# A decoder layer on eight cores: bf16 chunks at multiples of 64 bytes, and conditioning blocks spread through the merge

## What is computed

```
ada = silu(c) @ w_ada + b_ada            # shift1, scale1, gate1, shift2, scale2, gate2
h   = rmsnorm(x, g_pre1) * (1 + scale1) + shift1
z   = h @ w_in                           # pool 1024 | lru 2048 | pool gate 2048 | lru gate 2048
y_pool = (window mean - u_pool) @ w_grp * scale ; y_lru = rglru(causal conv(u_lru))
merged = sigmoid(g_pool) * (y_pool @ w_pool_up) + sigmoid(g_lru) * (y_lru @ w_lru_up)
x   = x + gate1 * rmsnorm(merged @ w_out, g_post1)
h   = rmsnorm(x, g_pre2) * (1 + scale2) + shift2
up  = causal conv3(h @ w_ffn_up)         # 2 x 6144
x   = x + gate2 * rmsnorm((gelu(up_gate) * up_value) @ w_ffn_down, g_post2)
```

## Time and profile before

| | |
|---|---|
| time of three runs | 2472.26, 2476.87, 2477.47 us |
| the profiled execution | 2471.48 us |
| its span, slowest core (core 4) | 2469.9 us |
| spans of the eight cores | 2461.9 to 2469.9 us |
| PE busy | 2202.4 us (89%) |
| DVE, ACT busy | 1067.3 us (43%), 916.7 us (37%) |
| bytes moved by DMA | 338.42 MB, 137 GB/s |

### The profile page before, as it was taken

How to read it: one execution, slowest core, us unless ns; L and a number is a source line. 1 busy time by engine, 2 the same in 40 slices (tenths; PEclk the granted TensorE clock), 3 DMA queues, 4 the chain that set the end, 5 groups by cost and what they waited for, 6 DMA issues and landing times.

```text
span 2469.9 us, 41807 instructions; the slowest of 8 cores (2461.9 to 2469.9 us)
## 1 busy us (share of the span) xinstructions
PE 2202.4 (89%) x16574; PEld 1136.6 (46%) x16896; DVE 1067.3 (43%) x2195; ACT 916.7 (37%) x1232; POOL 146.5 (6%) x281
## 2 busy tenths in 40 slices
PE   2447888898888999999899999999999999999995
PEld 0122444444444555555445555555555555555552
DVE  0356988997311111111337666540005776563003
ACT  2446878885200000002364455440104444442101
POOL 0000000000000000000000000000000000000000
PEclk8568999999999999999999999999999999999997
DMA  9994656564265555658989976669877996778983
GB/s 226 250 163 77 107 100 110 90 114 96 52 111 101 105 94 96 110 104 148 180 177 192 187 142 130 128 131 184 132 128 146 199 172 134 137 137 162 199 134 96
DMA packets 61967, 338.42 MB, mean 137 GB/s; under 512 B 7504, under 2 KB 8016, under 8 KB 28240
## 3 DMA queue, kind: packets, MB, share of 16 engines
q0 software_dynamic: 39888, 273.17, 63.7%
q1 hardware_dynamic: 21888, 62.56, 7.8%
HBM read 586.69 MB, written 22.17 MB: 247 GB/s over the span
## 4 chain that ended last, share of the span: by engine, by line
PE 80%; ACT 7%; DMA 5%; DVE 5%; issue 3%; DVEq 0%; ACTq 0%; SPq 0%; POOLq 0%
PE ps_all L253 80%; ACT sb_R L230 6%; DMA sb_w<-w_ada 3%; DVE sb_R L236 2%; DVE sb_R L233 2%; DMA sb_R<-xp 1%; DMA sb_w<-w_lru_up 1%; ACT L230 1%; DVE sb_R L256 0%; ACT sb_rstd L230 0%; DVE sb_R L247 0%; DVEq L145 0%; ACT sb_wsm L230 0%; DVE sb_R L241 0%; DVE sb_mod L243 0%
## 5 line engine op out<-in xcount | busy, mean ns | idle before, releaser
L253 PE MATMUL ps_all<-sb_R,sb_w 128*128 128x512 bf16 (+4 forms) x14293 | 2032.8, 300 | 51.5 <-DMA sb_w<-w_lru_up 17.9
L253 PEld LDWEIGHTS ps_all<-sb_R,sb_w 128*128 128x128 bf16 x14592 | 1039.0, 98 | 1029.8 <-issue 62.9
L230 ACT ACTIVATE sb_R<-ps_all 128x128 f32<-128x128 f32 (+6 forms) x416 | 213.4, 546 | 662.3 <-PE ps_all L253 589.4
L236 DVE SCALAR_TENSOR_TENSOR sb_R<-sb_R,sb_cvec 128x450 f32<-128x450 f32 (+3 forms) x576 | 379.0, 703 | 26.8 <-ACT sb_R L230 15.2
L233 DVE TENSOR_TENSOR sb_R<-sb_R 128x577 bf16<-128x577 f32 (+9 forms) x148 | 166.0, 1121 | 169.5 <-ACT sb_R L230 153.2
L230 ACT ACTIVATE sb_R<-sb_R 128x578 f32<-128x578 f32 (+9 forms) x216 | 207.2, 981 | 78.3 <-DMA sb_R<-xp 44.1
L230 ACT ACTIVATE sb_wsm<-ps_all 128x577 bf16<-128x577 f32 (+1 forms) x64 | 42.0, 656 | 431.7 <-PE ps_all L253 431.2
L230 ACT ACTIVATE sb_R<-ps_all,sb_cvec 128x577 f32<-128x577 f32 (+4 forms) x184 | 170.4, 928 | 22.3 <-DVE sb_R L233 15.3
L233 DVE TENSOR_TENSOR sb_R<-sb_R,sb_mod 128x128 f32<-128x128 f32 x96 | 27.9, 290 | 297.8 <-ACT sb_R L230 294.5
L243 DVE TENSOR_SCALAR sb_mod<-ps_all,sb_cvec 128x17 f32<-128x17 f32 x96 | 18.0, 228 | 318.3 <-PE ps_all L253 317.6
L233 DVE TENSOR_TENSOR sb_R<-sb_R,sb_rstd 128x577 f32<-128x577 f32 (+5 forms) x128 | 119.9, 961 | 9.3 <-ACT sb_rstd L230 9.3
(11 more groups left out here) (57 smaller groups left out, 702.2 us busy)
## 6 DMA issues: line engine op xcount, KB each, us to landing
sb_w<-w_ffn_up POOLq DMA_DIRECT2D x96, 1024.0 KB, 9.9
sb_w<-w_ada POOLq DMA_DIRECT2D x48, 1024.0 KB, 15.4
sb_w<-w_ffn_down POOLq DMA_DIRECT2D x48, 1024.0 KB, 10.4
sb_w<-w_in POOLq DMA_DIRECT2D x36, 1024.0 KB, 11.3
sb_w<-w_out POOLq DMA_DIRECT2D x16, 1024.0 KB, 10.2
sb_R<-xm SPq DMA_DIRECT2D x4, 2312.0 KB, 91.9
sb_R<-xp SPq DMA_DIRECT2D x4, 2048.0 KB, 42.3
sb_w<-w_lru_up POOLq DMA_DIRECT2D x8, 1024.0 KB, 7.7
```

The costliest lines, as they stand in the source:

```text
L230: return self.P.op("act", lambda e: e.activation(out=out, in_=in_, func=func, **kw), after)
L236: return self.P.op("dve", lambda e: e.scalar_tensor_tensor(out=out, in0=in0, scalar=scalar, in1=in1, op0=op0, op1=op1), after)
L253: return self.P.op("pe", lambda e: e.matmul(out, lhsT=lhsT, rhs=rhs, start=start, stop=stop), after, signal)
```

## The change

Three edits.

1. Every bf16 view gets a stride that is a multiple of 64 bytes: SNB = 1184 elements (2368 bytes) in place of 1156, and SBB = 608 elements (1216 bytes) in place of 578. The offsets of the arena are moved so that all bf16 views start at multiples of 64; `R` itself moves to the front of SBUF (byte 16768 = 64 x 262) with the weight slots and `sb_wsm` behind it, all at multiples of 64. fp32 views keep their strides. The one operand that does not start at 64 is half B in the output projection: it reads `merged` from column 577, so at 2 bytes past a multiple of 64 (before: at 2 or 10 bytes past a multiple of 16). 256 of the 5120 pairs are of that kind.
2. To make room, `hist_up` moves into the tile `sth`, whose store to DRAM then has to be done first (`t_sth_out` is added to the waits of FFN up A, and `ffree` to those of the copies into `hist_up`), and of the four `x1s` buffers three instead of two lie in the first region.
3. In the merge, one ada block is run before the second gates block of a round, and one (two in round 3) between `w_lru_up` and `w_pool_up`, in place of three or two in a row behind the gates. In all it is 17 blocks as before.

```
+SNB = 1184
+SBB = 608
 O_HM = 0
-O_XM = O_HM + 4 * SN
+O_XM = 5568
+O_AG = 16 * 2 * SNB
+O_WGRP = O_AG + 8 * 4 * SN
+O_YLRU = O_WGRP + 4096
...
-O_YLRU = O_HP
...
+for o_bf in (O_HM, O_YLRU, O_HP, O_SQ, O_XCB, O_DB, O_YPOOL, O_MERGED, O_H2A, O_H2B, O_FLO, O_FHI):
+    assert o_bf % 64 == 0
...
+            self.R = self.sb("R", [128, R_BYTES // 4], F32)
+            self.wslots = [self.sb("w%d" % i, [128, 16, 256], BF16) for i in range(4)]
+            self.wsm = [self.sb("wsm%d" % i, [128, 2, 2, 256], BF16) for i in range(2)]
...
-            self.hist_up = self.sb("hist_up", [128, 96, 2], F32)
...
+            self.hist_up = self.sth[:].rearrange("p c s -> p (c s)")[:, 0:192].rearrange("p (c t) -> p c t", t=2)
...
-        hm = self.bfv(O_HM, 16, SN)
+        hm = self.bfv(O_HM, 16, SNB)
...
-        merged = self.bfv(O_MERGED, 16, SN)
+        merged = self.bfv(O_MERGED, 16, SNB)
...
+            self.ada_step()
             tg.update(self.gates(12 + q, 0, prev))
-            self.ada_step(3 if q < 2 else 2)
...
                     self.release(b, 3, [tg[bi + j]])
+                if bi:
+                    self.ada_step(2 if q == 3 else 1)
...
-                      h2=self.bfv(O_H2A, 16, SB_), halo=HALO, y0=0, t_g=[None] * DK, t_d=[None] * DK),
+                      h2=self.bfv(O_H2A, 16, SBB), halo=HALO, y0=0, t_g=[None] * DK, t_d=[None] * DK),
...
-        f_lo = self.bfv(O_FLO, 32, SB_)
-        f_hi = self.bfv(O_FHI, 16, SB_)
+        f_lo = self.bfv(O_FLO, 32, SBB)
+        f_hi = self.bfv(O_FHI, 16, SBB)
...
-                        keep.append(self.Vcopy(self.hist_up[:, chn, :], U[:, npr:npr + 2], evs[gv]))
+                        keep.append(self.Vcopy(self.hist_up[:, chn, :], U[:, npr:npr + 2], evs[gv] + ffree))
...
-        ftA = ffn_up("A", Ring([0, 2, 4]), nB, lambda jf: 1, [self.t_merge, halves["A"]["t_o"], self.t_stl_out])
+        ftA = ffn_up("A", Ring([0, 2, 4]), nB, lambda jf: 1, [self.t_merge, halves["A"]["t_o"], self.t_stl_out, self.t_sth_out])
...
-        x1s = [self.f32(O_X1ST + i * 4 * SB_, SB_) for i in range(2)]
-        x1s += [self.f32(O_X1SU + i * 4 * SB_, SB_) for i in range(2)]
+        x1s = [self.f32(O_X1ST + i * 4 * SB_, SB_) for i in range(3)] + [self.f32(O_X1SU, SB_)]
```

More of the change, by code:

```diff
@@ L51 @@
 O_SQ = O_XP + 16 * 4 * SP_
-O_AG = 16 * 2 * SN
-O_WGRP = O_AG + 8 * 4 * SN
-O_YLRU = O_HP
 SU = 1208
-O_U = O_YLRU + 16 * 2 * SN
+O_U = O_YLRU + 16 * 2 * SNB
 O_XC = O_U + 2 * 4 * SU
 O_XCB = O_XC + 4 * 4 * SN
-R_BYTES = O_XCB + 4 * 2 * SN
-O_YPOOL = O_AG + 4 * 4 * SN
 O_STP = O_AG
-O_DB = O_AG + 2 * 4 * SN
+O_DB = O_STP + 8 * SEQS * 15 * 4
+O_YPOOL = O_WGRP - 8 * 2 * SNB
 PU = 15 + NPR + SEQS * 23
-O_PU = O_YLRU + 16 * 2 * SN
+O_PU = O_U
 O_PS = O_PU + 4 * 4 * PU
 O_GB = O_AG
-O_MERGED = O_YLRU + 16 * 2 * SN
+O_GB3 = O_YPOOL - 4 * SN
+O_MERGED = O_U
+R_BYTES = O_MERGED + 16 * 2 * SNB
 O_OA = 0
@@ L70 @@
 O_H2A = 2 * 16 * 4 * SB_
-O_H2B = O_H2A + 16 * 2 * SB_
+O_H2B = O_H2A + 16 * 2 * SBB
 NXST = 6
-O_XST = O_H2B + 2 * 2 * SB_
-O_FLO = O_MERGED
+O_XST = O_H2B + 2 * 2 * SBB
+O_FLO = R_BYTES - 32 * 2 * SBB
 O_FHI = 0
 FU = 612
-O_FU0 = 16 * 2 * SB_
+O_FU0 = 16 * 2 * SBB
 O_D = O_OB
@@ L80 @@
 O_X1ST = O_STF + 96 * 32 * 4
-O_X1SU = O_H2B + 16 * 2 * SB_
+O_X1SU = O_H2B + 16 * 2 * SBB
 O_X1B = O_H2A
[L83 to L88, removed]
+for o_bf in (O_HM, O_YLRU, O_HP, O_SQ, O_XCB, O_DB, O_YPOOL, O_MERGED, O_H2A, O_H2B, O_FLO, O_FHI):
+    assert o_bf % 64 == 0
+for k_hm in range(16):
+    assert O_HM + 2 * SNB * (k_hm + 1) <= O_XM + 4 * SN * (k_hm // 2)
+assert O_SQ + 2 * 2 * SNB <= R_BYTES and O_XCB + 4 * 2 * SNB <= R_BYTES
+assert O_HP + 16 * 2 * SP_ <= O_U
+assert O_DB + 2 * 2 * SNB <= O_GB3 and O_PS + 2 * 4 * PU <= R_BYTES
+assert O_GB + 2 * 4 * SN <= O_GB3
+assert O_XST + NXST * 4 * SB_ <= O_X1SU and O_X1SU + 4 * SB_ <= O_MERGED and O_X1SU + 4 * SB_ <= O_FLO
+assert O_X1ST + 3 * 4 * SB_ <= O_H2B and O_X1B + 16 * 4 * SB_ <= O_FLO
 class Prog:
@@ L353, in build @@
             self.sth = self.sb("sth", [128, 16, SEQS], F32)
-            self.R = self.sb("R", [128, R_BYTES // 4], F32)
-            self.wslots = [self.sb("w%d" % i, [128, 16, 256], BF16) for i in range(4)]
+            self.hist_up = self.sth[:].rearrange("p c s -> p (c s)")[:, 0:192].rearrange("p (c t) -> p c t", t=2)
             self.w_sem = [P.new_sem("wsem%d" % i) for i in range(4)]
@@ L360, in build @@
             self.w_rot = 4
-            self.wsm = [self.sb("wsm%d" % i, [128, 2, 2, 256], BF16) for i in range(2)]
             self.wsm_sem = [P.new_sem("wsmsem%d" % i) for i in range(2)]
@@ L446, in front @@
         self.t_dv = self.Vts(self.dv[:, 3, :], self.dv[:, 2, :], 0.5, None, ALU.mult, after=[tv])
-        sq = [self.bfv(O_SQ + i * 2 * SN, 1, SN)[:, 0, :] for i in range(2)]
+        sq = [self.bfv(O_SQ + i * 2 * SNB, 1, SNB)[:, 0, :] for i in range(2)]
         sq_free = [None, None]
         hp = self.bfv(O_HP, 16, SP_)
-        hm = self.bfv(O_HM, 16, SN)
+        hm = self.bfv(O_HM, 16, SNB)
         self.hp, self.hm = hp, hm
@@ L597, in lru @@
         xc = [self.f32v(O_XC + s * 2 * 4 * SN, 2, SN) for s in range(2)]
-        xcb = [self.bfv(O_XCB + s * 2 * 2 * SN, 2, SN) for s in range(2)]
+        xcb = [self.bfv(O_XCB + s * 2 * 2 * SNB, 2, SNB) for s in range(2)]
         av = [self.f32v(O_AG + s * 4 * 4 * SN, 2, SN) for s in range(2)]
         gv = [self.f32v(O_AG + s * 4 * 4 * SN + 2 * 4 * SN, 2, SN) for s in range(2)]
-        y_lru = self.bfv(O_YLRU, 16, SN)
+        y_lru = self.bfv(O_YLRU, 16, SNB)
         self.y_lru = y_lru
@@ L795, in lru @@
         self.store(self.o_lh_p, self.h_carry[:], self.t_lru)
-        self.store(self.o_lh_s, self.sth[:], self.t_lru)
+        self.t_sth_out = self.store(self.o_lh_s, self.sth[:], self.t_lru)
     def pool_first(self, half_free, rows_free):
@@ L806, in pool_first @@
         S = [self.f32(O_PS + s * 4 * PU, PU) for s in range(2)]
-        db = self.bfv(O_DB, 2, SN)
+        db = self.bfv(O_DB, 2, SNB)
         stp = self.f32(O_STP, 8 * SEQS * 15).rearrange("p (c s t) -> p c s t", c=8, s=SEQS)
-        y_pool = self.bfv(O_YPOOL, 8, SN)
+        y_pool = self.bfv(O_YPOOL, 8, SNB)
         self.y_pool = y_pool
@@ L934, in merge_first @@
     def merge_first(self):
-        self.gb = [self.f32(O_GB, SN), self.f32(O_GB + 4 * SN, SN), self.rstd[:], self.f32(O_GB + 3 * 4 * SN, SN)]
+        self.gb = [self.f32(O_GB, SN), self.f32(O_GB + 4 * SN, SN), self.rstd[:], self.f32(O_GB3, SN)]
         self.merge_ring = Ring([0, 3])
@@ L1006, in ffn @@
         xst_cnt = [0] * NXST
-        sqn = self.bfv(O_H2B, 2, SB_)
+        sqn = self.bfv(O_H2B, 2, SBB)
         sqm = {"buf": sqb, "i": 0, "free": [None, None]}
@@ L1237, in ffn_up @@
                 H["stf_out"] = self.store(self.o_fconv_s, stf, H["t_up"])
-                self.store(self.o_fconv_p, self.hist_up[:], H["t_up"])
+                self.store(self.o_fconv_p, self.hist_up, H["t_up"])
             return ft
```

2 lines of the change are left out of this document (1 added, 1 removed).

## The result

| | before | after |
|---|---|---|
| median of four runs, us | 2475.09 (2472.26 to 2477.47) | 2441.21 (2438.84 to 2444.10) |
| ratio, 95% interval | | 0.9864 (0.9847 to 0.9881) |
| spans of the eight cores, us | 2461.9 to 2469.9 | 2427.1 to 2442.5 |

The account below looks back on a forecast made before the run. PE was taken as the bound (80% of the chain), by matmul cost and two merge stalls. Alignment 33.5 us plus merge order 21.8 made 55.3 us off, forecast 2420 us, range 2409 to 2434.

Parts of the forecast that it names:

- the 1.8 ns: PE matmuls with aligned operands: each costs 1.8 ns beyond its columns at 2.4 GHz, so about 244 ns a pair.
- 2.6 as the bound: Pessimistic extra cost per aligned matmul, 2.6 ns, read from `hp`; it lowers the alignment gain from 33.5 to 20.8 us.
- The term of 25.3 us for the FFN: FFN up and down: 4608 pairs, each 5.5 ns faster once aligned, save 25.3 us (bound 17.0).
- the triples: Matmul triples of 1155 columns, 896 of them in the merge: 5.8 ns less each when aligned, 5.2 us there (bound 3.0).
- output projection A: Output projection of half A: 256 pairs at 3.3 ns less each, 0.8 us saved.
- the recurrence: Main pass of the recurrence: 256 aligned triples save 1.5 us, or 0 if PE's waits for ACT swallow it.
- Rival C: FFN: faster PE wants weights earlier than DMA lands them, so PE stalls and the clock falls; 2480 us or more, chance 0.03.
- The tight place in round 3: Merge: the gates load of round 4 has 9.6 us of cover; if it lands in 10.6, PE waits 1.0 us.
- the costs at nothing: No added instructions, ACT and DVE durations unchanged (within 1 us), and the added waits on the store of `sth` cost 0.
- Rival B: Merge: stalls only move, through late loads or a lower clock; 2431 us if half the 21.8 returns, 2442 if all; chance 0.07.
- Rival A: PE matmuls: cost is fixed per matmul, not by address, so alignment gives 0; 2455 us, chance 0.08 (mostly its weak form).
- its weak form: Aligned matmuls keep a floor of 2.6 ns, so alignment gives 20.8 us in place of 33.5: 2434 us.

Follow-up runs that it names:

- half-pace version: Changed kernel with half A's closing work (x re-reads, y stores) advanced at every second output chunk of FFN up B: 2434.5 us, again 2434.9 (ratio 0.9841).
- Two thirds of the pace: Changed kernel with half A's closing work advanced at two of three output chunks of FFN up B: 2435.5 us, ratio 0.9842 (two runs).

## Why the prediction was right or wrong

**The step that failed first is the 1.8 ns.** "I take the 1.8, since pairs and squares run in the same stretch and shape, and keep 2.6 as the bound." The 243 to 244 ns of the earlier trace rows and the short steps of the earlier trace rows are real, but they belong to an aligned pair right behind an off one: 244.2 with 0 and 8 off in turn, 246.5 in a run of aligned pairs. The squares show it too: behind off chunks each took 244 to 245 ns, after the change some take 250. `hp` in the earlier trace rows was the only one of the rows of before with nothing but aligned chunks, and it gave 2.6. By it the FFN pair comes to 246.0, 0.5 too low. The term of 25.3 us for the FFN is 4608 x (249.6 - 246.5) = 14.3, and the triples gain 3.4 ns instead of 5.8. With the other terms at their bounds (20.8 - 17.0 = 3.8) edit 1 comes to 18.1, where 33.5 stood; 19.8 was measured without late re-reads. That is 14 us short. Of the smaller terms, output projection A gained 0.2 us where 0.8 stood, and the recurrence nothing clear where 1.5 stood: on the six cores with full records its main pass took from 1.0 us less to 1.5 more.

The formula of the Trainium skill that I held against the address ("TensorE: Matmul & The Clock Gate", section Back-to-back issue gap, N / 2.4 + 2.5 ns) gives 245.4 for the aligned pair, 488.8 for the triple and 430.4 for the pair of `hp`; measured are 246.5, 489.1 and 430.8. Where all chunks are aligned it holds within 1.1 ns; it has no term for the 1.3 to 3.4 ns that offsets add. The same section of the Trainium skill calls this the isolated gap and gives about 131 ns for N = 512 in a stream with weight loads; here every matmul of such a stream with 512 columns takes 215.0 ns or more, so the measurement speaks for the formula.

**The second is cover that was taken for free.** Rival C asked whether a faster PE asks for more than the DMA engines move, and looked only at the weights, with a share of 0.80 over the whole FFN. In the 90 us of the re-reads the share was 0.99 before the change, and the landings already grew to 36 us, which only a stretch cut to that stage shows. After it PE stood behind them, and the clock fell, as in C, at another load and at a sixth of its price: 8.7 us, shown by the pace. That the faster PE is what made them later, C's trigger, is not shown.

**Edit 3 was right**: 21.8 forecast, 21 measured alone, no wait and no low clock between 663 and 780. The tight place in round 3 showed, at 1.48 us on core 1 where 1.0 was priced. **Edit 2 and the costs at nothing** show no cost in the rows, though no run has edit 2 alone: PE has no wait for a load in FFN up A, and DVE's convolution takes 818 and 819 ns (817 and 818 in the earlier trace rows), here grouped by output tile in FFN up A:

```profile
L243 DVE SCALAR_TENSOR_TENSOR sb_R<-sb_R,sb_cvec 128x577 f32<-128x577 f32 x131 | 106.8, 818 | 7.2 <-DVE sb_R L243 0.5
L243 DVE SCALAR_TENSOR_TENSOR sb_stl<-sb_R,sb_cvec,sb_stl 128x577 f32<-128x577 f32 x44 | 36.0, 819 | 2.3
```

**The sum again**: 21.0 for the merge and 19.8 for the layout are 40.8, less 8.7 for the late re-reads 32.1; measured 33.9. The terms come from different chips and from few runs, so agreement within 2 us is as much as they can show. The half-pace version, with nothing late, gained 39.

**Rival B** is refuted for the merge, but for the 1.5 us of round 3. **Rival A** in its strong form, that the address costs nothing, is refuted by 249.6 against 246.5; its weak form was the true size and had deserved more than a part of 0.08. By it and the late re-reads the forecast would have been near 2443.

## What to carry to other kernels

Take the cost of an operation from a stretch that holds nothing else, the way it will run after the change; the fast member of a mixed sequence may be fast because its neighbours are slow. Keep the chunks of a moving operand at one offset from 16 bytes, best at 0: from 249.6 ns a pair, one offset for all (4, 8 or 12) gave 1.8, offset 0 another 1.3. Before speeding up an engine, read the DMA share of each stage with its own window, and the landing times in order: where they grow from one transfer to the next and come near the time that the buffers give (here 32 us, with stalls from some 39 on), thin out the background transfers first.

## What was not expected of the hardware

- Aligning only every second chunk gains nothing: 248.0 ns a pair with 0 and 8 off in turn, 247.8 with all of them 8 off. Four classes in turn are dearest (249.6).
- Offset 2 is dearer than 4, 8 or 12: output projection B, all its chunks 2 bytes off after the change, takes 249.4 ns a pair of 578 columns, and took 249.5 with chunks 2 and 10 off in turn. FFN up B, also with 578 columns, takes 247.8 with all chunks 12 off. It is another stage, and no run moves its offset alone.
- Two thirds of the pace is enough: a DMA share of 0.94 still gave landings under 15 us, 0.99 let them grow by 2 to 4 us per transfer, before and after the change.
